# The second input projection of a two-layer backbone: two context tiles moved between the eight input tiles, and the vector rows waited for one by one

## The reference, cut to what matters

```python
x = layer_norm(RES_ALPHA * x + g2 * f, ln2_g[layer], ln2_b[layer])      # end of layer 0
ctx = layer_norm(RES_ALPHA * ctx + cg2 * fc, ln2_g[layer], ln2_b[layer])
...
h = modulate(x, sh1, sc1)                                               # start of layer 1
hc = modulate(ctx, csh1, csc1)
a, q, k, v, p, u, g = split_projection(h @ w_in)                        # 1536 columns
kvc = hc @ w_in[:, COL_K:COL_POOL]                                      # 256 columns only
```

## Time and profile before

| | us |
|---|---|
| median of 3 executions | 2620.19 |
| lowest, highest | 2618.93, 2623.39 |
| the profiled execution | 2621.88 |
| its span, first to last instruction | 2619.9 |
| mean granted TensorE clock in it | 0.946 of full speed |

### The profile page before, as it was taken

The page is one execution under the profiler, slowest core; times in us unless marked ns, Lnnn a source line. Parts: engine busy times, 40 slices in busy tenths (PEclk is TensorE's granted clock), DMA queues, the critical chain, the costliest instruction groups (busy, mean ns, idle before and its releaser), DMA issues. The chain is left out here.

```text
span 2619.9 us, 38975 instructions
## 1 busy us (share of the span) xinstructions
PE 2350.8 (90%) x15056; PEld 1638.6 (63%) x15056; DVE 943.7 (36%) x2274; ACT 405.7 (15%) x1055; POOL 467.5 (18%) x608
## 2 busy tenths in 40 slices
PE   4999769998499999999959997899579999999996
PEld 3999745564466666666639994555356666666652
DVE  1777735666411011101116565566611111111114
ACT  0110133331011111111101113233100000000000
POOL 0000013454011111111111111244111111111111
PEclk8999889999599999999979998899789999999998
DMA  9555430001498999999932102200099999999955
GB/s 353 187 166 172 147 113 9 25 17 57 176 352 329 386 400 388 390 394 394 368 117 101 49 33 101 77 17 25 29 392 381 383 382 396 386 387 398 372 235 210
DMA packets 131438, 608.98 MB, mean 232 GB/s; under 512 B 21408, under 2 KB 24480, under 8 KB 112912
## 3 DMA queue, kind: packets, MB, share of 16 engines
q1 hardware_dynamic: 113328, 569.88, 56.3%
q0 software_dynamic: 16864, 37.78, 3.8%
q10 hardware_dynamic: 1152, 0.03, 0.0%
HBM read 599.67 MB, written 42.04 MB: 245 GB/s over the span
## 5 line engine op out<-in xcount | busy, mean ns | idle before, releaser
L1987 PEld LDWEIGHTS gate_up<-room,w_gate_up 128*128 128x128 f32 x4608 | 521.1, 193 | 31.6 <-issue 31.6
L1987 PE MATMUL gate_up<-room,w_gate_up 128*128 128x128 f32 x4608 | 527.9, 277 | 3.2 <-DVE room L1869 3.2
L1996 PE MATMUL down<-w_down,room 128*128 128x512 f32 x576 | 256.8, 599 | 0.0
L2004 PE MATMUL gate_up_short<-w_gate_up,room 128*64 128x512 f32 x1152 | 255.1, 595 | 0.0
L1878 DVE TENSOR_TENSOR room<-room,gate_up 128x128 f32<-128x128 f32 x144 | 41.4, 288 | 538.9 <-ACT room L1908 538.9
L2004 PEld LDWEIGHTS gate_up_short<-w_gate_up,room 128*64 128x64 f32 x1152 | 79.5, 137 | 171.2 <-issue 171.2
L1996 PEld LDWEIGHTS down<-w_down,room 128*128 128x128 f32 x576 | 106.5, 190 | 123.0 <-issue 120.5
L1599 POOL COPY rows_idx<-slot_token 128x1 int32 (+1 forms) x78 | 14.4, 185 | 784.5 <-PE rows_turned L1974 721.8
L1886 DVE TENSOR_TENSOR room<-room,gate_up_short 128x256 f32<-128x256 f32 x36 | 15.2, 421 | 369.1 <-ACT room L1915 369.1
L2017 PE MATMUL down<-w_down,room 128*64 128x512 f32 x576 | 131.5, 598 | 11.9 <-ACT room L1917 11.9
L1404 PE MATMUL proj<-w_out,mixT 128*128 128x512 f32 x288 | 129.5, 592 | 0.0
(11 more groups left out here) (360 smaller groups left out, 3234.3 us busy)
## 6 DMA issues: line engine op xcount, KB each, us to landing
w_gate_up<-in_w_exp_gate SPq DMA_DIRECT2D x72, 2048.0 KB, 8.7
w_gate_up<-in_w_exp_up SPq DMA_DIRECT2D x72, 2048.0 KB, 13.4
w_down<-in_w_exp_down SPq DMA_DIRECT2D x72, 2048.0 KB, 12.2
ada_w<-in_w_ada SPq DMA_DIRECT2D x96, 512.0 KB, 5.1
h_rows<-h SPq DMA_DIRECT2D x18, 512.0 KB, 2.6
w_out<-in_w_out SPq DMA_DIRECT2D x2, 4096.0 KB, 13.5
w_in<-in_w_in SPq DMA_DIRECT2D x2, 3072.0 KB, 18.1
xn<-expert_rows SPq DMA_DIRECT2D x10, 512.0 KB, 3.9
```

The source lines that it names most:

```text
L1987: mm = nc.tensor.matmul(H[j % 2][:, o, :], wgu[0][:, o, k, j * P:(j + 1) * P], xT[0][:, k, :], start=k == 0, stop=k == KT - 1)
L1996: mm = nc.tensor.matmul(Y[:, h, :], hid[:, j, :], wd[0][:, j, h * 512:(h + 1) * 512], start=j == 0, stop=j == JT - 1)
L2004: mm = nc.tensor.matmul(Hs[c * HP:(c + 1) * HP, :, :], xT[1][:, k, :], wgu[1][:, :, k, c * 2 * P:(c + 1) * 2 * P], start=k == 0, stop=k == ...
```

## The change

The tiles are taken in the order 0, 1, 2, 8, 3, 4, 5, 9, 6, 7 by every engine, with `i` the place in that order and `t` the tile. Buffers and semaphore counts go by place; `nth(i)` counts the latent tiles ahead of place i, for the semaphores that only latent tiles raise. Nothing is added to or taken from the arithmetic. The one semaphore for the three vector rows becomes two, and each wait moves behind the instructions that don't need the row: the one for `g2` to just ahead of the multiplication in `combine`, the one for `ln2_g` and `ln2_b` to just ahead of the operation that uses them. The context tiles' wait for their own `g2` moves in the same way.

```diff
-def combine(nc, v, s, g, t, ya, yb, g2, lng, lnb, r, used, dst):
+def combine(nc, v, s, g, t, n, ya, yb, g2, lng, lnb, r, used, rows_for):
 
     x = g.x[:, t, :]
     nc.vector.scalar_tensor_tensor(ya, yb, g.gate[:, t, 1:2], ya, ALU.mult, ALU.add).then_inc(used, 1)
-    v.wait_ge(used, t + 1)
+    v.wait_ge(used, n + 1)
+    if rows_for[0]:
+        v.wait_ge(*rows_for[0])
     nc.vector.tensor_tensor(ya, ya, g2, ALU.mult).then_inc(s.sem, s.up())
...
     rows_stats(nc, v, s, ya, r)
-    v.wait_ge(r.var_ready, t + 1)
+    v.wait_ge(r.var_ready, n + 1)
+    if rows_for[1]:
+        v.wait_ge(*rows_for[1])
     nc.vector.scalar_tensor_tensor(ya, ya, r.mv[:, 0:1], lng, ALU.subtract, ALU.mult).then_inc(s.sem, s.up())
...
+        ORDER = [0, 1, 2, LT, 3, 4, 5, LT + 1, 6, 7]
+        nth = lambda i: sum(t < LT for t in ORDER[:i])
...
         def tiles(body):
 
-            for t in range(NT):
-                body(t, t % 2)
+            for i, t in enumerate(ORDER):
+                body(i, t, i % 2)
...
-                fetch = lambda t, q: fetch_experts(sp, g, t, xn[q][:, :], yb[q][:, :], landed[q])
-
-                def step(t, q):
-                    if not (t >= NT - 2):
-                        sp.wait_ge(used, t + 1)
-                        sp.wait_ge(turned, t + 1)
-                        fetch(t + 2, q)
+                fetch = lambda i, q: fetch_experts(sp, g, ORDER[i], xn[q][:, :], yb[q][:, :], landed[q])
+
+                def step(i, t, q):
+                    if i < NT - 2:
+                        sp.wait_ge(used, i + 1)
+                        sp.wait_ge(turned, i + 1)
+                        fetch(i + 2, q)
...
-                sp.dma_start(g2[:, 0, :], g2_of(0)).then_inc(vec_ld, 16)
+                sp.dma_start(g2[:, 0, :], g2_of(0)).then_inc(g2_ld, 16)
                 for j, n in enumerate(("ln2_g", "ln2_b")):
-                    sp.dma_start(ln2[:, j, :], a[n][l - 1:l, :].to_broadcast([P, D])).then_inc(vec_ld, 16)
+                    sp.dma_start(ln2[:, j, :], a[n][l - 1:l, :].to_broadcast([P, D])).then_inc(ln_ld, 16)
...
-                def normalise(t, q):
-                    v.wait_ge(gated, t + 1)
-                    if t == 0:
-                        v.wait_ge(vec_ld, 48)
-                    if stream(t):
-                        v.wait_ge(g2c_ld, 16)
-                    combine(nc, v, s, g, t, xn[q][:, :], yb[q][:, :], g2[:, stream(t), :], ln2[:, 0, :], ln2[:, 1, :],
-                            c_norm, used, None).then_inc(s.sem, s.up())
+                def normalise(i, q):
+                    t = ORDER[i]
+                    v.wait_ge(gated, i + 1)
+                    rows_for = ((g2c_ld, 16) if stream(t) else (g2_ld, 16) if i == 0 else None), ((ln_ld, 32) if i == 0 else None)
+                    combine(nc, v, s, g, t, i, xn[q][:, :], yb[q][:, :], g2[:, stream(t), :], ln2[:, 0, :], ln2[:, 1, :],
+                            c_norm, used, rows_for).then_inc(s.sem, s.up())
...
-                def step(t, q):
-                    last = t == NT - 1
-                    if not last:
-                        modulate(t + 1, 1 - q)
-                    if not (t >= NT - 2):
-                        normalise(t + 2, q)
-                    v.wait_ge(c_done, t + 1)
+                def step(i, t, q):
+                    if i < NT - 1:
+                        modulate(i + 1, 1 - q)
+                    if i < NT - 2:
+                        normalise(i + 2, q)
+                    v.wait_ge(c_done, i + 1)
...
-                        v.wait_ge(d_done, t + 1)
+                        v.wait_ge(d_done, nth(i) + 1)
...
-                        v.wait_ge(a_free, t + 2)
+                        v.wait_ge(a_free, nth(i) + 2)
                         sg = m.sg[:, t, :]
-                        rows_norm(nc, v, s, sg, sg, v_norm, t).then_inc(s.sem, s.up())
+                        rows_norm(nc, v, s, sg, sg, v_norm, nth(i)).then_inc(s.sem, s.up())
```

More of the change, by code:

```diff
@@ L226, in combine @@
     rows_stats(nc, v, s, ya, r)
-    v.wait_ge(r.var_ready, t + 1)
+    v.wait_ge(r.var_ready, n + 1)
+    if rows_for[1]:
+        v.wait_ge(*rows_for[1])
     nc.vector.scalar_tensor_tensor(ya, ya, r.mv[:, 0:1], lng, ALU.subtract, ALU.mult).then_inc(s.sem, s.up())
     v.wait_ge(s.sem, s.at())
-    v.wait_ge(r.rstd_ready, t + 1)
-    return nc.vector.scalar_tensor_tensor(dst if dst is not None else x, ya, r.rstd[:, :], lnb, ALU.mult, ALU.add)
+    v.wait_ge(r.rstd_ready, n + 1)
+    return nc.vector.scalar_tensor_tensor(x, ya, r.rstd[:, :], lnb, ALU.mult, ALU.add)
 def take_wait(pool, waited):
@@ L648, in normalise, with modulate @@
                     v.wait_ge(s.sem, s.at())
                     x = g.x[:, t, :]
-                    rows_norm(nc, v, s, x, xn[q][:, :], x_norm, t).then_inc(xn_ready, 1)
-                def modulate(t, q):
-                    v.wait_ge(turned, t + 1)
+                    rows_norm(nc, v, s, x, xn[q][:, :], x_norm, i).then_inc(xn_ready, 1)
+                def modulate(i, q):
+                    t = ORDER[i]
+                    v.wait_ge(turned, i + 1)
                     for k in range(4, KT):
-                        i = nc.vector.tensor_scalar(hT[q][:, k, :], T[:, k, :], g.cols[:, l, stream(t), 1, k:k + 1],
+                        op = nc.vector.tensor_scalar(hT[q][:, k, :], T[:, k, :], g.cols[:, l, stream(t), 1, k:k + 1],
@@ L656, in modulate, with step @@
                                                     g.cols[:, l, stream(t), 0, k:k + 1], ALU.mult, ALU.add)
[L657 to L665 removed]
+                    op.then_inc(mod_v, 1)
+                def step(i, t, q):
+                    if i < NT - 1:
+                        modulate(i + 1, 1 - q)
+                    if i < NT - 2:
+                        normalise(i + 2, q)
+                    v.wait_ge(c_done, i + 1)
@@ L688, in _, with modulate, gating, step @@
             def _(act):
-                def modulate(t, q):
-                    act.wait_ge(turned, t + 1)
+                def modulate(i, q):
+                    t = ORDER[i]
+                    act.wait_ge(turned, i + 1)
                     for k in range(4):
-                        i = nc.scalar.activation(hT[q][:, k, :], T[:, k, :], ACT.Identity,
+                        op = nc.scalar.activation(hT[q][:, k, :], T[:, k, :], ACT.Identity,
                                                  bias=g.cols[:, l, stream(t), 0, k:k + 1], scale=g.cols[:, l, stream(t), 1, k:k + 1])
[L694 to L700, removed]
+                    op.then_inc(mod_a, 1)
+                def gating(i, q):
+                    act.wait_ge(landed[q], (i - q) * 16 + 32)
+                    nc.scalar.activation(xn[q][:, :], xn[q][:, :], ACT.Copy, scale=g.gate[:, ORDER[i], 0:1]).then_inc(gated, 1)
+                def step(i, t, q):
                     if not kv_only(t):
-                        act.wait_ge(a_done, t + 1)
+                        act.wait_ge(a_done, nth(i) + 1)
                         nc.scalar.activation(m.u[:, :, at_tile(t)], A[:, 0:GW].rearrange("p (j n) -> p j n", j=2), ACT.Gelu)
                         nc.scalar.activation(m.sg[:, t, :], A[:, GW:2 * GW], ACT.Gelu).then_inc(a_free, 1)
-                    act.wait_ge(b_done, t + 1)
+                    act.wait_ge(b_done, i + 1)
                     vb = 1 if not stream(t) else 2
@@ L709, in step @@
                     nc.scalar.activation(m.v[:, t + vb, :], B[:, GW:GW + P], ACT.Copy).then_inc(b_free, 1)
[L710 to L713, removed]
+                    if i < NT - 1:
+                        modulate(i + 1, 1 - q)
+                    if i + 2 < NT:
+                        gating(i + 2, q)
                 act.nop().then_inc(a_free, 1)
@@ L723, in _, with turn, step @@
             def _(pe):
-                def turn(t, q):
-                    pe.wait_ge(xn_ready, t + 1)
+                def turn(i, q):
+                    pe.wait_ge(xn_ready, i + 1)
                     for k in range(KT):
-                        i = nc.tensor.transpose(T[:, k, :], xn[q][:, k::KT], g.k[:, K_ID:K_ID + P])
-                    i.then_inc(turned, 1)
+                        tr = nc.tensor.transpose(T[:, k, :], xn[q][:, k::KT], g.k[:, K_ID:K_ID + P])
+                    tr.then_inc(turned, 1)
                 def run(out, lhsT, rhs):
                     for k in range(KT):
[L732 to L737, removed]
+                        mm = nc.tensor.matmul(out, lhsT(k), rhs(k), start=k == 0, stop=k == KT - 1)
+                    return mm
+                def step(i, t, q):
+                    pe.wait_ge(mod_a, i + 1)
+                    pe.wait_ge(mod_v, i + 1)
                     h = hT[q]
                     if not kv_only(t):
-                        pe.wait_ge(a_free, t + 1)
+                        pe.wait_ge(a_free, nth(i) + 1)
                         pe.wait_ge(ug_ld, 16)
@@ L749, in step @@
```

(6 more changed lines are left out.)

20 lines of the change are left out of this document (10 added, 10 removed).

## The result

| | before | after |
|---|---|---|
| median | 2621.46 us (2618.93 to 2624.45) | 2626.28 us (2623.05 to 2630.11) |
| profiled execution | 2621.88 us, span 2619.9 | 2626.73 us, span 2625.0 |
| granted TensorE clock | 0.946 | 0.944 |

Twelve executions of each: the ratio is 1.0017 with a 95% interval of 1.0009 to 1.0024. By the medians the change makes the kernel 4.8 us slower. That is within 0.2%, but the whole interval lies on the slow side. Forecast were 4.1 us more and 2624.3 us.

The account below looks back on a forecast made before the run. PE was taken to bound the stage between latent tiles. Its end: 1559.36 - 3.3 + 20.28 - 1.05 + 2.2 = 1577.5 against 1573.4, so 4.1 us later: 2624.3 us, range 2620 to 2629.5.

Parts of the forecast that it names:

- the likeliest case: Whole kernel: the forecast as summed, 2622 to 2627 us, at 73%; by kind, within 0.2% of before, at 0.62.
- The head: Start of the stage: line 220 no longer waits for vector rows and starts at 1361.3, a gain of 3.3 us.
- The context tiles: Between latent tiles: each takes 10.14 us from `bankB` to the next step, with a 3.78 us pause; two take 20.28.
- I take the fall after each new pause to be like the one seen: Clock behind both new pauses: falls as in the trace of before, with bounds of -0.3 and +2.4 us.
- the second rival: Behind both pauses: clock stays low into the next latent tile, `bankA` 6.13 for 3.74; 8.9 us later, 2629.1 us; 13%.
- That leaves 0.7 us, so I take no second wait.: Latent step after a context tile: `xn` is ready at 1580.9, PE asks at 1581.6, so PE doesn't wait.
- The last step: End of the stage, now a latent tile: no `turn`, 1.05 us less, but copy and gate's norm, 2.2 us more.
- No `turn`, which takes off 1.05 us: Last latent step of the stage: it has no `turn` inside, so it is 1.05 us shorter.
- The copy and norm: After the last latent tile's `bankD`: DVE's copy and the gate's norm take 2.2 us, where a context tile has 0.29.
- the tiles hide in DVE's slack: Rival, context tiles between latent ones: each costs only 4.95 us, the stage ends 6.3 us sooner, 2613.9 us; 4%.
- The head's gain: Start of the stage: 3.3 us sooner; the rival that it doesn't arrive gave 7.4 us later, 2627.6 us, at 8%.
- this trace agrees: Clock after the one old pause: the trace was said to agree with the skill's warning of throttled bursts after waits.

Follow-up runs that it names:

- waits_only: Kernel of before, in its old tile order, with only the change's two moved waits; 2618.41 us, ratio 0.9984.
- join_between_2: Changed kernel with `normalise` cut, its first three DVE operations and ACT's gating one step earlier, `bankC` and `bankD` freed ahead of that; 2615.51 us, ratio 0.9969.
- one_between: Changed kernel with order 0, 1, 2, 8, 3, 4, 5, 6, 7, 9: one context tile between, one last; 2615.97 us, ratio 0.9977.
- order_only: Changed kernel with the vector-row waits back at the top of tile 0 and of the context tiles; 2628.69 us, ratio 1.0028.

## Why the prediction was right

**The result** lies in the range, and the likeliest case is the one that happened. The medians moved by 4.8 us for a forecast of 4.1. In the profiles the stage is 225.38 - 219.30 = 6.1 us longer, and 4.7 longer than in the second profile of before. So the terms below were each right to about 1 us, and that the total came within 0.7 is in part luck. The 0.2% that the prediction took as the least that can be told from no change was too coarse: the interval of twelve executions is 0.09 to 0.24%.

**The head.** The mechanism was right in every part: ACT releases line 220, both rows have landed when they are needed, the weights are not late. The profile gives 2.5 us, waits_only 3.1 by medians, and profiles with a first fetch as quick as that of before 3.1 to 3.4. The first fetch landed 0.8 us later here, and in the second profile of before it was 1.0 later than in the first. So the 0.8 is not the change's.

**The context tiles.** The pause was forecast as 3.78 us and is 3.77 to 3.79 in every profile shown that has it. The 10.14 us were measured as 10.92 and 10.04. The step that was mis-sized is "I take the fall after each new pause to be like the one seen". Behind the first pause the clock was already low for `turn` (1.97 us against 1.25) and stayed low through `bankC`, which ended at 1458.0. DVE's `modulate` had ended at 1456.68, so PE's own matmuls set the start of the next step, 1.1 us behind `modulate`; in the trace of before that was 0.36 us. The step came 0.8 us later for it, and `bankA` took 0.2 more (3.96 against 3.74). Of the second rival, which had 2.39 us more in `bankA`, this is the beginning and no more. Behind the second pause `bankC` took 2.70 us, and the next step began 0.25 us after `modulate`.

**"That leaves 0.7 us, so I take no second wait."** No wait came, but it was close: line 214 ended at 1546.43 and `turn` started at 1546.58. I had let `normalise` start when `modulate` ends. Line 220 at 1534.60 waited 0.53 us for ACT's gating, which stands behind ACT's own `modulate`, and the working had left that out.

**The last step.** "No `turn`, which takes off 1.05 us" took the duration of eight pipelined transposes where their place in the row counts: 1437.06 to the next group at 1437.95, 0.89. The copy and norm were 2.24 for 2.2.

Together, for the first profile of before: 4.1 + 0.8 (head) + 0.9 (contexts, to the next `turn`: 23.40 and 22.30 for 22.40 each) + 0.2 (last step) + 0.1 (the first step) = 6.1. The whole span grew by 5.1: the stage began 0.55 us later and what follows it ran 1.5 us shorter (1044.1 us for 1045.6). Neither belongs to the change, as the thirteen profiles here spread from 1042.3 to 1045.6 behind the stage.

**The rivals.** That the tiles hide in DVE's slack did not happen, and for the reason given: join_between_2, which moves work from behind `modulate` to ahead of it, is the kernel in which they do hide, 6.6 us below before where that rival's sum said 6.3. The head's gain did arrive. The warning of the Trainium skill (TensorE: Matmul & The Clock Gate, HAM oscillation — how this bites in real kernels), that each wait between short bursts makes the next burst start throttled, held for both pauses here: `turn` took 1.97 us behind each, against 1.05 in a latent step. For the trace of before the prediction said too much in "this trace agrees". There the burst began at nearly full clock and fell about 1 us later:

```profile
1564.90:1566.00 1.10, 1.07 (x9) 1.08 (x10) 1.10 (x6) 0.00 (x0) 0.00 (x0) 0.94 0.00 0
```

What the low clock cost depends on how late DVE is anyway: at most 1.3 us at the first new pause (1.1 behind `modulate` and 0.2 in `bankA`) and 0.25 at the second, where `modulate` would have held PE until nearly the same time.

**Not settled**: whether one_between is truly a little better than waits_only; why the kernels with the two freeing lines moved gained some 3 us and not 0.5 to 1.4; what makes the first fetch land up to 1 us later in some executions; and where most of the scatter between executions of one kernel arises (2616.53 to 2627.43 us for before in the first batch). No trace here shows what sets the moment at which the clock falls.

## What to carry to other kernels

When a stage is bound by one engine, moving a short step into the middle helps only if the other engines have its successor ready by then. Work out what the fed engine has to do between two requests (10.7 us from one `turn` to the next at a context tile, 21.0 at a latent one) and what the feeders need for the answer (14.5 us from a turned tile to the next one normalised). Idle time of the feeder counts only at the place in its program order where it falls: here three operations of DVE and one of ACT, moved across one wait, were worth more than a third buffer, and the end of the stage was the cheapest place for a tile that leaves nothing to clean up. A second wait split off the first cost nothing that a row shows and gained some 3 us at the head of this stage, but look at what each engine's program has queued behind anything that is moved there.

## What the runs showed of the hardware that I had not expected

The same pause is not followed by the same clock. After five pauses of 3.78 to 3.79 us ahead of `turn`, the eight transposes took 1.25 us (before), 1.87 (before, second profile), 1.97 and 1.97 (after) and 1.97 (order_only), and the following sixteen matmuls of a context tile's `bankC` 3.53, 2.90, 3.62, 2.70 and 3.58 us, against 1.05 and 1.95 at full clock. From the first transpose to the next step it was 4.41, 4.41, 5.18, 4.31 and 5.18 us. And the stage began at 1354.99 us in one profile of before and at 1358.80 in the other: a spread of 3.8 us ahead of the change, almost as large as its whole effect, which is why a profile of each kernel says less of 4 us than the timed executions do.
